# A fused decoder trunk on one core: the pooling chunk of the input projection moved among the attention tasks

## The chip, the cores and the metric

The kernel runs on one core of a Trainium2 chip. Its time is device microseconds (us) of that core for one launch, from host arrays to the finished output. Five engines work side by side, each through its own queue in program order: TensorE (PE, matrix products and transposes), VectorE (DVE), ScalarE (ACT), GpSimd (POOL) and SyncE (SP, which issues the transfers). They meet only at semaphores.

## What is computed

Two layers over a sequence of 512 with width 1024, all in float32. The part that matters here is one layer's mixer:

```python
proj = jnp.einsum('btd,dn->btn', x, w_in[l])
(qa, ka, va, u, qc, kcm, vcm, ksl, vsl, kwi, vwi, gc) = jnp.split(proj, offsets, axis=-1)
...
o_a = diff_attention(qa[:, :, 0], qa[:, :, 1], ka[:, :, 0], ka[:, :, 1], va, lam, lam_init, subln_g[l])
o_b = pool_mixer(u, w_pool[l], pool_scale[l])
qc = apply_rope(qc...); kcm = apply_rope(...); ksl = apply_rope(...); kwi = apply_rope(...)
o_c = nsa_attention(qc, kcm, _to_kv(vcm, B, T), ksl, _to_kv(vsl, B, T), kwi, _to_kv(vwi, B, T), gates, ...)
mix = jnp.einsum('btm,md->btd', jnp.concatenate([o_a, o_b, o_c], axis=-1), w_out[l])
x = layer_norm(ALPHA * x + mix, ln1_g[l], ln1_b[l])
```

Behind it stands a squared-ReLU MLP of width 4096 with its own layer norm. Mixer A is differential attention (queries `qa`, keys `ka`, values `va`), mixer B averages `u` over windows of 2 to 16 rows and multiplies by a small matrix, mixer C is attention with a compressed, a selected and a window branch.

## The kernel before

**Products.** Every large product is made of three TensorE products of high and low parts (lines 650 to 652, in the MLP's "up" also 646 to 648), so that float32 accuracy is kept. Weights come in units of 256 rows. SP loads a unit into a ring of four (`raw`), ScalarE writes its high part (`w_hi`, line 936), GpSimd the low part (`w_lo`, line 506), and TensorE gives the place free (`unit_used`) when it has used it. A chunk is four units, that is a block of columns against all 1024 rows, 96 matrix instructions for the four row tiles.

**Projection.** The input projection has seven chunks: the queries of A, the keys of A (384 columns each), the compressed keys and values of C (274 columns), the queries of C (384), the values of A (384), `u` (256), and a last chunk of 512 columns (the remaining keys and values of C and the gates). Six of them run back to back; the last one is cut in eight pieces of 12 instructions that stand between the first nine tasks of mixer A (`last_chunk`). ScalarE copies each chunk's banks out (`copy_in`, lines 973 and 980), VectorE turns the rotary embedding (`rotate`, lines 402 to 412): first queries and keys of A, then the compressed keys, then the queries of C.

**Early transposes.** `turn_early` (line 827) transposes eight 128-column pieces for later use, four of them halfway through the chunk of A's values, four halfway through the chunk of `u`. It waits for the rotations (`roped_a`, `roped_m`). ScalarE copies four of the results (line 988), VectorE four (line 1261). GpSimd then lays out rows for the compression (`rows_to_compress`, line 539).

**Tasks.** 36 tasks follow, 18 of A and 18 of C. For task t TensorE writes the scores of task t+2 (lines 691 to 705), turns the probabilities (`turn_p`, line 717) and multiplies with the values (lines 738, 753). VectorE takes the maximum (line 1271) and scales (lines 1301 to 1319), ScalarE does the exponentials (line 1060) and copies the turned probabilities (line 1069). A table `SIDE` says at which task which small step runs: compression, further transposes, the windows of mixer B (`box`), its small matrix (`pool`), the sums of squares, the compressed scores. ScalarE and VectorE empty these from PSUM at the next task, and every engine takes its queue strictly in order.

## Time and profile before

| | us |
|---|---|
| median of 3 runs | 1332.22 |
| lowest and highest | 1332.1, 1334.91 |
| the profiled execution | 1336.63 |
| its span, first to last instruction | 1334.8 |

All times below are read from the one profiled execution, from its span's start. The two layers do the same work; the second one's mixer comes about 660 us after the first one's, so that a place in the first layer stands for its twin.

### The profile page before, as it was taken

The numbers are of one execution on the slowest core, as the hardware profiler recorded it, in microseconds if no ns is written. First come the engines' busy times: TensorE is split into PE (matmuls) and PEld (weight loads), VectorE is DVE, ScalarE is ACT, GpSimd is POOL, SyncE is SP. The second block draws the span as 40 slices with busy tenths as digits, with TensorE's granted clock in tenths as the row PEclk, the third lists the DMA queues.
The fourth block names the chain that finished last, engine by engine and source line by source line (L and its number), as shares of the span: only waits on it lengthen the run. The fifth ranks groups of instructions, "written<-read, shape, count | busy, mean of one in ns | idle before, by whom it ended". The sixth has DMA issues, their size and how long they took to land.

```text
span 1334.8 us, 17810 instructions
## 1 busy us (share of the span) xinstructions
PE 1273.2 (95%) x7090; PEld 1048.9 (79%) x7090; DVE 741.3 (56%) x1115; ACT 482.3 (36%) x960; POOL 538.4 (40%) x300
## 2 busy tenths in 40 slices
PE   7999989998999999999989999899989999999996
PEld 7997755678888888888889967556888888888885
DVE  4485578448865072360486755884487632614516
ACT  5324567533322122221233345775323322212221
POOL 4464122043644444444354722210554444444444
PEclk9998999999999999999989999999999999999998
DMA  7432002031432323333134220010324323232311
GB/s 245 124 82 77 1 1 64 2 126 33 158 95 95 96 101 104 95 95 91 36 98 128 83 64 0 16 50 0 126 77 139 100 96 95 95 95 96 101 57 63
DMA packets 68833, 110.08 MB, mean 82 GB/s; under 512 B 15056, under 2 KB 27664, under 8 KB 68624
## 3 DMA queue, kind: packets, MB, share of 16 engines
q1 hardware_dynamic: 67600, 104.77, 25.4%
q10 hardware_dynamic: 1152, 4.19, 0.9%
q8 instruction: 56, 0.92, 0.3%
q14 instruction: 25, 0.20, 0.1%
HBM read 106.85 MB, written 2.10 MB: 82 GB/s over the span
## 4 chain that ended last, share of the span: by engine, by line
PE 89%; DVE 7%; ACT 2%; POOL 1%; DMA 0%; issue 0%; POOLq 0%; SPq 0%; DVEq 0%; ACTq 0%
PE ps L650 17%; PE ps L651 16%; PE ps L652 16%; PE ps L646 9%; PE ps L647 9%; PE ps L648 9%; PE ps L705 4%; PE ps L717 2%; PE ps L753 2%; DVE negmax L1271 1%; PE ps L605 1%; DVE probs L1319 1%; PE ps L738 1%; DVE xres L1180 1%; PE ps L779 1%; DVE probs_a L1319 1%
## 5 line engine op out<-in xcount | busy, mean ns | idle before, releaser
L506 POOL TENSOR_TENSOR w_lo<-raw,w_hi 128x1024 fp32r<-128x1024 f32 (+3 forms) x200 | 461.7, 2315 | 635.5 <-ACT w_hi L936 635.2
L936 ACT ACTIVATE w_hi<-raw 128x1024 fp32r<-128x1024 f32 (+3 forms) x200 | 198.3, 994 | 601.9 <-PE ps L652 363.2
L646 PE MATMUL ps<-xt_hi,w_lo 128*128 128x512 f32 (+1 forms) x576 | 212.1, 368 | 8.8 <-DVE xt_lo L1161 8.8
L648 PE MATMUL ps<-xt_lo,w_hi 128*128 128x512 f32 (+1 forms) x576 | 211.8, 368 | 0.0
L647 PE MATMUL ps<-xt_hi,w_hi 128*128 128x512 f32 (+1 forms) x576 | 211.7, 368 | 0.0
L650 PE MATMUL ps<-w_hi,xt_lo 128*128 128x384 f32 (+3 forms) x448 | 153.5, 343 | 7.8 <-DVE xt_lo L1161 4.4
L650 PE MATMUL ps<-w_hi,mt_lo 128*128 128x512 f32 x384 | 150.6, 392 | 3.8 <-DVE mt_lo L1324 3.0
L651 PE MATMUL ps<-w_hi,xt_hi 128*128 128x384 f32 (+3 forms) x448 | 150.2, 335 | 0.0
L652 PE MATMUL ps<-w_lo,xt_hi 128*128 128x384 f32 (+3 forms) x448 | 150.0, 335 | 0.0
L652 PE MATMUL ps<-w_lo,mt_hi 128*128 128x512 f32 x384 | 149.5, 389 | 0.0
L651 PE MATMUL ps<-w_hi,mt_hi 128*128 128x512 f32 x384 | 149.4, 389 | 0.0
L646 PEld LDWEIGHTS ps<-xt_hi,w_lo 128*128 128x128 f32 x576 | 109.7, 190 | 27.2 <-DVE xt_lo L1161 8.1
L648 PEld LDWEIGHTS ps<-xt_lo,w_hi 128*128 128x128 f32 x576 | 109.9, 191 | 17.3
L647 PEld LDWEIGHTS ps<-xt_hi,w_hi 128*128 128x128 f32 x576 | 109.7, 190 | 17.5
L1271 DVE TENSOR_REDUCE negmax<-ps 128x2 f32<-128x256 f32 (+2 forms) x96 | 76.8, 820 | 67.3 <-PE ps L705 67.1
L1378 DVE TENSOR_TENSOR xres<-xres,ps 128x512 f32<-128x512 f32 x48 | 32.9, 685 | 137.4 <-PE ps L652 136.6
L650 PEld LDWEIGHTS ps<-w_hi,xt_lo 128*128 128x128 f32 x448 | 86.2, 192 | 21.3 <-issue 11.0
L650 PE MATMUL ps<-w_hi,he_lo 128*128 128x512 f32 x256 | 99.6, 389 | 0.0
L651 PE MATMUL ps<-w_hi,he_hi 128*128 128x512 f32 x256 | 99.6, 389 | 0.0
L652 PE MATMUL ps<-w_lo,he_hi 128*128 128x512 f32 x256 | 99.6, 389 | 0.0
L1406 DVE TENSOR_TENSOR mt_lo<-tmp,mt_hi 128x512 fp32r<-128x512 f32 x32 | 71.3, 2229 | 47.9 <-ACT mt_hi L1136 47.9
L1414 DVE TENSOR_SCALAR tmp<-ps 128x512 f32<-128x512 f32 x64 | 44.1, 689 | 89.6 <-PE ps L648 88.5
(167 smaller groups left out, 1937.7 us busy)
## 6 DMA issues: line engine op xcount, KB each, us to landing
raw<-in_w_up SPq DMA_DIRECT2D x64, 512.0 KB, 3.7
raw<-in_w_down SPq DMA_DIRECT2D x64, 512.0 KB, 3.7
raw<-in_w_in SPq DMA_DIRECT2D x32, 384.0 KB, 3.3
raw<-in_w_in SPq DMA_DIRECT2D x8, 512.0 KB, 3.6
raw<-in_w_out SPq DMA_DIRECT2D x8, 512.0 KB, 3.3
raw<-in_w_out SPq DMA_DIRECT2D x12, 256.0 KB, 3.7
raw<-in_w_in SPq DMA_DIRECT2D x8, 274.0 KB, 2.9
xres<-in_x SPq DMA_DIRECT2D x4, 512.0 KB, 5.6
```

The source lines that it names most:

```text
L506: nc.gpsimd.tensor_tensor(unit_of(w_lo, u), unit_of(raw, u), unit_of(w_hi, u).bitcast(F32), ALU.subtract).then_inc(s_lo_ready, 1)
L646: mm(o, wl[:, c], a_hi[:, k, cols], start=first, stop=False)
L647: mm(o, wh[:, c], a_hi[:, k, cols], start=False, stop=False)
L648: return mm(o, wh[:, c], a_lo[:, k, cols], start=False, stop=end)
L650: mm(o, a_lo[:, k, c], wh, start=first, stop=False)
L651: mm(o, a_hi[:, k, c], wh, start=False, stop=False)
L652: return mm(o, a_hi[:, k, c], wl, start=False, stop=end)
L705: last = mm(o[:, at_:at_ + n], queries, keys, start=False, stop=True, skip_group_check=True)
L936: A(unit_of(w_hi, u), unit_of(raw, u), ACT.Copy).then_inc(s_hi_ready, 1)
L1271: last = V.tensor_reduce(negmax[:, t % 2, a, :], ps[:, b:b + 2, at_:at_ + n], AX.X, ALU.max, negate=True)
L1406: V.tensor_tensor(lo[:, f], tmp[:, f % 2], hi[:, f].bitcast(F32), ALU.subtract) \
L1414: link(V.tensor_scalar(tmp[:, f % 2], ps[:, bank + b, :], 0.0, None, ALU.max))
```

## The change

The chunk of `u` is no longer part of the run of chunks ahead of the tasks. The 512-column chunk (now `LATE`) comes as the sixth, cut into eight pieces, of which two now stand between the first two scores. The chunk of `u` (now `POOLED`) comes as the seventh, one row tile each at tasks 11, 13, 15 and 16. Since five chunks are left in the run, the early transposes move one chunk ahead. The steps of mixer B (`box`, `pool`) move from tasks 6 and 12 to tasks 18 to 22, one bank each. ScalarE empties `pool` and the sums of squares in VectorE's place, and takes the scale and the small constant into the logarithm. The compression runs as 32 products of 64x64 in place of 16 of 128x128.

```diff
-IN_COLS = ((0, 384), (384, 384), (O_KCM, 274), (O_QC, 384), (O_VA, 384), (O_U, 256), (O_KCM + 274, 512))
+IN_COLS = ((0, 384), (384, 384), (O_KCM, 274), (O_QC, 384), (O_VA, 384), (O_KCM + 274, 512), (O_U, 256))
-LAST = IN_CHUNKS - 1
+LATE, POOLED = IN_CHUNKS - 2, IN_CHUNKS - 1
+LATE_AT = {1: (1, 0), 2: (1, 1), 4: (2, 0), 5: (2, 1), 7: (3, 0), 8: (3, 1)}
+LATE_COPIED = {0: 0, 3: 1, 6: 2, 9: 3}
+POOLED_AT, POOLED_COPIED = {11: 0, 13: 1, 15: 2, 16: 3}, {12: 0, 14: 1, 16: 2, 17: 3}
...
+SIDE = {2: (("compress", 0, 5), ("turn", 7, 6)), 4: (("turn", 8, 5), ("turn", 9, 6)),
+        6: (("cmp_scores", 0, 5), ("cmp_scores", 1, 6)), 8: (("square_sums", 0, 5),), 12: (("turn", 11, 5), ("turn", 12, 6)),
+        14: (("cmp_turn", 0, 5), ("cmp_turn", 1, 6)), 16: (("square_sums", 1, 5),), 18: (("box", 0, LATE_BANK),),
+        19: (("box", 1, LATE_BANK),), 20: (("square_sums", 2, LATE_BANK),), 21: (("pool", 0, LATE_BANK),),
+        22: (("pool", 1, LATE_BANK),)}
...
# TensorE
-                    for j in range(16):
-                        last = mm(ps[:, bank, 0:P], cmp_wv[:, j].rearrange("p a e -> p (a e)"),
-                                  cmp_kw[:, j].rearrange("p a e -> p (a e)"), start=j == 0, stop=j == 15)
+                    for j in range(16):
+                        for kv in range(2):
+                            r = slice(64 * kv, 64 * kv + 64)
+                            last = mm(ps[r, bank, r], cmp_wv[:, j, kv, :], cmp_kw[:, j, kv, :], start=j == 0, stop=j == 15)
...
+            def pooled_tile(layer, b):
+                pe.wait_ge(s_in_copied, nth("in_copied", layer, TT * POOLED + b))
+                for k in range(KT):
...
+                    last = products(POOLED, k, b, LATE_BANK - b, xt_hi, xt_lo)
...
-                        gemm(layer, s, 4 * (k % 2), xt_hi, xt_lo, lambda kt: None, by_bank=k == LAST - 1,
-                             halfway=(lambda: turn_early(layer, k - 4)) if k >= 4 else None)
+                        gemm(layer, s, 4 * (k % 2), xt_hi, xt_lo, lambda kt: None, by_bank=k == LATE - 1,
+                             halfway=(lambda: turn_early(layer, k - 3)) if k >= 3 else None)
...
+                pe.wait_ge(s_in_copied, nth("in_copied", layer, TT * (LATE - 1) + 2))
                 scores(layer, 0)
+                late_piece(layer, 0, 0)
+                pe.wait_ge(s_in_copied, nth("in_copied", layer, TT * LATE))
                 scores(layer, 1)
+                late_piece(layer, 0, 1)
...
# ScalarE
-                    if 20 <= t < 24:
-                        split_to(layer, U_OUT + t - 19)
+                    if t in (20, 24, 28, 32):
+                        split_to(layer, U_OUT + t // 4 - 4)
...
+                    if t == 9:
+                        split_to(layer, U_OUT)
...
-                A(flat, flat, ACT.Ln).then_inc(s_chain_act, 1)
+                A(flat, flat, ACT.Ln, scale=1.0 / DV, bias=lams[:, 7:8]).then_inc(s_chain_act, 1)
...
# VectorE
+                copy_early(2)
+                copy_early(3)
                 dve.wait_ge(s_in_copied, nth("in_copied", layer, 4 * TT))
                 for tt in range(TT):
                     rotate(V.tensor_tensor, link, tt, ((T_QC, 6, 64, R_CCQ, R_SCQ),)).then_inc(s_roped_c, 1)
...
-                for n in (2, 3, 4, 6):
...
+                copy_early(4)
+                copy_early(6)
```

TensorE's queue at the first early transposes, in the first layer (before: rows 442 to 448 of the queue, in the chunk of A's values):

```order
L650 MATMUL ps<-w_hi,xt_lo 128x384
L651 MATMUL ps<-w_hi,xt_hi 128x384
L652 MATMUL ps<-w_lo,xt_hi 128x384
L827 MATMUL ps<-kc,proj_b 128x128 [waits in_copied,roped_m,roped_a]
L827 MATMUL ps<-kc,proj_b 128x128 x7
L827 MATMUL ps<-kc,proj_a 128x128 x8
L650 MATMUL ps<-w_hi,xt_lo 128x384 [waits hi_ready,lo_ready]
```

The same place after the change (rows 346 to 352, in the chunk of C's queries; the helper now has line 834):

```order
L658 MATMUL ps<-w_hi,xt_lo 128x384
L659 MATMUL ps<-w_hi,xt_hi 128x384
L660 MATMUL ps<-w_lo,xt_hi 128x384
L834 MATMUL ps<-kc,proj_b 128x128 [waits in_copied,roped_m,roped_a]
L834 MATMUL ps<-kc,proj_b 128x128 x7
L834 MATMUL ps<-kc,proj_a 128x128 x8
L658 MATMUL ps<-w_hi,xt_lo 128x384 [waits hi_ready,lo_ready]
```

The transposes and their wait for both rotations stand 96 matrix instructions, one chunk of 384 columns, earlier in the queue.

VectorE's queue from the last rotation of the compressed keys (`proj_b` 128x128) to the first score maximum, before:

```order
L412 TENSOR_TENSOR proj_b<-proj_b,tmp 128x384 [waits chain_dve]
L1261 COPY qa_64<-ps 128x512 [waits turned,roped_c]
L1261 COPY ka<-ps 128x512 [waits turned]
L1261 COPY qa_65<-ps 128x512 [waits turned]
L1261 COPY qa_66<-ps 128x512 [waits turned]
L1264 TENSOR_TENSOR lams<-lams 128x1 [waits lam_exp]
L1265 TENSOR_TENSOR lams<-lams,kc 128x1 [waits chain_dve]
L1271 TENSOR_REDUCE negmax<-ps 128x2 [waits scores,chain_dve]
```

And after, with the rotation of C's queries (`proj_b` 128x384, 16 rows) between the two pairs of copies:

```order
L419 TENSOR_TENSOR proj_b<-proj_b,tmp 128x128 [waits chain_dve]
L1295 COPY qa_65<-ps 128x512 [waits turned,roped_m]
L1295 COPY ka<-ps 128x512 [waits turned]
L409 TENSOR_TENSOR tmp<-proj_b,kc 128x6x32 [waits in_copied]
...
L419 TENSOR_TENSOR proj_b<-proj_b,tmp 128x384 [waits chain_dve]
L1295 COPY qa_66<-ps 128x512 [waits turned,roped_c]
L1295 COPY qa_67<-ps 128x512 [waits turned]
L1307 TENSOR_TENSOR lams<-lams 128x1 [waits lam_exp]
L1308 TENSOR_TENSOR lams<-lams,kc 128x1 [waits chain_dve]
```

Two copies now stand ahead of the rotation of C's queries, two behind it; the rotations of A's queries and keys and of the compressed keys keep their place.

ScalarE's queue at task 9 after the change, from the sums of squares to the exponentials of task 10 (`proj_k`, `proj_v`, `gates` are one row tile of the 512-column chunk, `w_hi` the four units of `u`):

```order
L1068 ACTIVATE rms<-ps 128x512 [waits side_ready]
L1007 ACTIVATE proj_k<-ps 128x110 [waits unit_used]
L1007 ACTIVATE proj_v<-ps 128x128
L1007 ACTIVATE proj_k<-ps 128x128
L1007 ACTIVATE proj_v<-ps 128x128
L1000 ACTIVATE gates<-ps 128x18
L963 ACTIVATE w_hi<-raw 128x2x256 [waits unit_used,raw0]
L963 ACTIVATE w_hi<-raw 128x2x256 [waits unit_used,raw1]
L963 ACTIVATE w_hi<-raw 128x2x256 [waits unit_used,raw2]
L963 ACTIVATE w_hi<-raw 128x2x256 [waits unit_used,raw3]
```

Before, no unit was split among the tasks of A; the sums of squares were VectorE's.

## Rows read from the trace of the kernel before

**Rows 1.** The page: engines' busy time, and the chain that ended last.

```profile
PE 1273.2 (95%) x7090; PEld 1048.9 (79%) x7090; DVE 741.3 (56%) x1115; ACT 482.3 (36%) x960; POOL 538.4 (40%) x300
...
PE 89%; DVE 7%; ACT 2%; POOL 1%; DMA 0%; issue 0%; POOLq 0%; SPq 0%; DVEq 0%; ACTq 0%
```

**Rows 2.** Windows: A's tasks in both layers, C's; PE first, PEclk after POOL.

```profile
110.30:197.20 86.90, 80.02 (x544) 55.66 (x542) 55.10 (x115) 46.84 (x156) 18.71 (x21) 0.94 0.07 19
197.20:254.40 57.20, 53.62 (x465) 32.73 (x465) 46.54 (x110) 45.16 (x116) 9.42 (x4) 1.00 0.13 38
770.60:855.90 85.30, 78.45 (x544) 54.84 (x542) 55.01 (x114) 46.79 (x156) 18.71 (x21) 0.96 0.07 20
```

**Rows 3.** TensorE's timeline, rows with idle time: start, us, engine, line, [idle <-releaser].

```profile
97.00 0.36 PE L650 MATMUL ps<-w_hi,xt_lo 128*128 128x256 f32 x1 [1.29 <-ACT proj_v L980]
...
114.52 0.34 PE L695 MATMUL ps<-mask,ident 128*128 128x128 bf16 x2 [1.77 <-ACT probs_a L1060]
...
189.44 1.32 PE L717 MATMUL ps<-kc,probs_a 128*128 128x128 f32 x6 [2.63 <-DVE probs_a L1317]
```

**Rows 4.** Windows: granted clock behind the wait of 1.77 us.

```profile
115.00:121.00 6.00, 6.00 (x15) 3.97 (x16) 4.07 (x11) 2.31 (x10) 0.65 (x1) 0.50 0.52 160
```

**Rows 5.** VectorE's timeline, rotations of the compressed keys, from its first row.

```profile
74.97 1.89 DVE L402 TENSOR_TENSOR tmp<-proj_b,kc 128x64 f32<-128x64 f32 x2
...
77.55 0.36 DVE L402 TENSOR_TENSOR tmp<-proj_b,kc 128x64 f32<-128x64 f32 x2
...
81.88 0.29 DVE L412 TENSOR_TENSOR proj_b<-proj_b,tmp 128x128 f32<-128x128 f32 x1
```

**Rows 6.** ScalarE's timeline: splits that mark used units, copies of C's queries.

```profile
69.06 0.85 ACT L936 ACTIVATE w_hi<-raw 128x768 fp32r<-128x768 f32 x1 [2.49 <-PE ps L652]
...
82.08 0.86 ACT L980 ACTIVATE proj_b<-ps 128x384 f32<-128x384 f32 x2
85.71 0.63 ACT L936 ACTIVATE w_hi<-raw 128x512 fp32r<-128x512 f32 x1 [2.77 <-PE ps L652]
```

**Rows 7.** GpSimd's timeline: a split beside the rotations, the next one.

```profile
69.99 1.87 POOL L506 TENSOR_TENSOR w_lo<-raw,w_hi 128x768 fp32r<-128x768 f32 x1 [2.11 <-ACT w_hi L936]
74.15 2.50 POOL L506 TENSOR_TENSOR w_lo<-raw,w_hi 128x768 fp32r<-128x768 f32 x1 [2.29 <-ACT w_hi L936]
```

**Rows 8.** TensorE's timeline: both early transposes, values of a task, the compression.

```profile
85.45 1.04 PE L827 MATMUL ps<-kc,proj_b 128*128 128x128 f32 x8
...
102.83 1.91 PE L827 MATMUL ps<-kc,proj_a 128*128 128x128 f32 x16
...
127.43 0.88 PE L738 MATMUL ps<-pt_a,proj_v 128*64 128x128 f32 x12
128.24 3.84 PE L779 MATMUL ps<-cmp_kw,cmp_wv 128*128 128x128 f32 x32
```

**Rows 9.** VectorE's timeline: a rotation of C's queries, and a copy behind it.

```profile
91.83 1.61 DVE L402 TENSOR_TENSOR tmp<-proj_b,kc 128x192 f32<-128x192 f32 x2
...
95.50 0.69 DVE L1261 COPY qa<-ps 128x512 f32<-128x512 f32 x1
```

**Rows 10.** ScalarE and TensorE: scores, exponentials, copies, transposes among tasks of A.

```profile
106.20 0.38 ACT L980 ACTIVATE proj_b<-ps 128x256 f32<-128x256 f32 x1 [0.83 <-PE ps L652]
...
132.55 1.13 PE L705 MATMUL ps<-ka,qa 32*128 32x512 f32 x4
133.48 0.68 ACT L1060 ACTIVATE probs_a<-ps,negmax 128x512 f32<-128x512 f32 x1
...
136.47 0.82 PE L717 MATMUL ps<-kc,probs_a 128*128 128x128 f32 x6
...
137.33 0.81 ACT L1069 ACTIVATE pt_a<-ps 128x768 f32<-128x768 f32 x1 [2.40 <-PE ps L717]
...
143.73 0.27 ACT L980 ACTIVATE proj_k<-ps 128x110 f32<-128x110 f32 x1
...
144.41 0.43 ACT L1060 ACTIVATE probs_a<-ps,negmax 128x128 f32<-128x128 f32 x1
```

More of the change, by code:

```diff
@@ L544, in _ @@
             for layer in range(DEPTH):
-                split(layer, 2 if layer else 0, U_LAST - 2)
+                split(layer, 2 if layer else 0, U_LATE - 2)
                 pool.wait_ge(s_const_in, 32)
@@ L570, in _ @@
                 rope_k(3)
+                split(layer, U_POOLED, U_OUT)
                 pool.wait_ge(s_cmp_factor, nth("cmp_factor", layer, 1))
@@ L828, in turn_early, with late_piece @@
                     last.then_inc(s_turned, 1)
-            def last_chunk(layer, t):
-                b = t // 3
-                if t % 3 == 0:
-                    pe.wait_ge(s_in_copied, nth("in_copied", layer, TT * LAST + b if b else TT * (LAST - 1) + 1))
-                for k in range(4 * (t % 3), 4 * (t % 3) + 4):
+            def late_piece(layer, b, half):
+                if b and not half:
+                    pe.wait_ge(s_in_copied, nth("in_copied", layer, TT * LATE + b))
+                for k in range(4 * half, 4 * half + 4):
                     if b == 0 and k % 2 == 0:
-                        pe.wait_ge(s_lo_ready, nth("lo_ready", layer, U_LAST + k // 2 + 1))
-                        pe.wait_ge(s_hi_ready, nth("hi_ready", layer, U_LAST + k // 2 + 1))
-                    last = products(LAST, k, b, LAST_BANK - b, xt_hi, xt_lo)
+                        pe.wait_ge(s_lo_ready, nth("lo_ready", layer, U_LATE + k // 2 + 1))
+                        pe.wait_ge(s_hi_ready, nth("hi_ready", layer, U_LATE + k // 2 + 1))
+                    last = products(LATE, k, b, LATE_BANK - b, xt_hi, xt_lo)
                     if b == 3 and k % 2:
@@ L842, in last_chunk @@
                     elif k == KT - 1:
-                        last.then_inc(s_last_done, 1)
+                        last.then_inc(s_late_done, 1)
+            def pooled_tile(layer, b):
+                pe.wait_ge(s_in_copied, nth("in_copied", layer, TT * POOLED + b))
+                for k in range(KT):
+                    if b == 0 and k % 2 == 0:
+                        pe.wait_ge(s_lo_ready, nth("lo_ready", layer, U_POOLED + k // 2 + 1))
+                        pe.wait_ge(s_hi_ready, nth("hi_ready", layer, U_POOLED + k // 2 + 1))
+                    last = products(POOLED, k, b, LATE_BANK - b, xt_hi, xt_lo)
+                    if b == 3 and k % 2:
+                        last.then_inc(s_unit_used, 1)
+                    elif k == KT - 1:
+                        last.then_inc(s_pooled_done, 1)
             pe.wait_ge(s_ident_in, 16)
@@ L849, in _ @@
                     turn_half(0, 0, 0)
-                for k, s in enumerate(range(LAST)):
+                for k, s in enumerate(range(LATE)):
                     if k >= 2:
@@ L887, in _ @@
                 for t in range(TASKS):
+                    if t == 16:
+                        pooled_tile(layer, POOLED_AT[t])
                     if t + 2 < TASKS:
                         scores(layer, t + 2)
-                    if t < 3 * TT and t % 3 < 2:
-                        last_chunk(layer, t)
+                    if t in LATE_AT:
+                        late_piece(layer, *LATE_AT[t])
+                    if t in POOLED_AT and t != 16:
+                        pooled_tile(layer, POOLED_AT[t])
                     if t == TASKS - 1:
@@ L994, in _ @@
                 act.wait_ge(s_const_in, 32)
-                for n in range(1, U_LAST - 1):
+                for n in range(1, U_LATE - 1):
                     if n == 4:
@@ L1039, in side_step @@
                         last = A(cmp_pt[0:64, 2 * c:2 * c + 2, 1, :], src[0:64, :, 1, :], ACT.Copy)
+                    elif kind == "square_sums":
+                        last = A(rms[:, c], b, ACT.Copy)
+                    elif kind == "pool":
+                        last = A(pooled[:, c], b, ACT.Identity, scale=psc[:, c:c + 1], bias=lams[:, 6:7])
                     elif kind == "box":
@@ L1220, in _ @@
             V.memset(lams[:, 6:7], 0.0)
+            V.memset(lams[:, 7:8], RMS_EPS)
             V.memset(kcmp[:], 0.0)
@@ L1276, in side @@
                     for n, (kind, c, bank) in enumerate(SIDE[t]):
-                        if kind in ("cmp_scores", "square_sums", "pool"):
+                        if kind == "cmp_scores":
                             dve.wait_ge(s_side_ready, nth("side_ready", layer, SIDE_FIRST[t] + n + 1))
```

131 lines of the change are left out of this document (64 added, 67 removed).

## The prediction

> **What bounds the kernel now.** I read the page first: TensorE is busy for 95% of the span and makes 89% of the chain that ended last [rows 1]. The reader is to see that no other engine is near it, so a change pays only where TensorE waits or runs slow. Then the windows of the stretch that is touched. The tasks of A take 86.9 us in the first layer with TensorE busy for 80.0, and 85.3 with 78.5 in the second; the tasks of C take 57.2 with 53.6 [rows 2]. So 6.9 us of waiting per layer stand in A and 3.6 in C. The granted clock there averages 0.94 and 0.96 [rows 2]: 0.06 x 86.9 = 5.2 us and 0.04 x 85.3 = 3.4 us of lost speed. A window shows where it goes: the clock stands at 0.50, the 1.2 GHz level, from 115 to 121 [rows 4], right behind a wait of 1.77 us for the exponentials of the first task [rows 3], 3.0 us lost; the other 2.2 us fit the other long wait, 2.63 us, where VectorE is late with task 15 [rows 3]. One wait stands ahead of the tasks, 1.29 us before the chunk of `u` [rows 3]. The row names ScalarE; by the wait's list and the time it is VectorE's second copy behind the rotation, which starts 0.6 us after the copy at 95.50 [rows 9]. All that the change can win, if it wins all of A and the wait ahead of it, is 6.9 + 5.2 + 1.3 = 13.4 us in the first layer and 6.9 + 3.4 + 1.3 = 11.6 in the second, 25.0 in all; C has 3.6 more per layer.
>
> **What moves at no price.** The chunk of `u` is 96 instructions; half of it runs from 97.00 to 102.83 [rows 3, 8], so it is 11.7 us of TensorE, taken from the projection and given to the tasks: nothing on a full TensorE except what it covers. The same holds for `box` and `pool`, which move to C. VectorE's five evacuations go to ScalarE, which is busy for 46.8 of 86.9 us in A and 45.2 of 57.2 in C [rows 2]; I cost them at nothing in C, where TensorE gets 4 us of new work to cover them, and take up to 2 us per layer either way for the range. The compression takes 3.8 us for 32 instructions, 0.12 each; with a 64-column operand the values' products take 0.81 to the next row for 12, 0.07 each [rows 8], and 64 of them are 4.3 us, while pairs that ran fully side by side at half the width would be 1.9. I take no change, and -1.9 to +0.5 per layer for the range. The scale in the logarithm, the later splits of the output weights and the transfers (whose order by unit stays) lie beside TensorE's work: nothing.
>
> **The cost: the early transposes come before their rotations are done.** They now stand halfway through the chunk of C's queries. The unit ahead of them was used at 69.06, where ScalarE's split starts, and the transposes start about 0.26 ahead of such a split (85.45 against 85.71), so TensorE arrives at 68.8 [rows 6, 8]. They wait for both rotations. VectorE, whose order up to there is the same, starts the compressed keys only at 74.97 and ends them at 82.17 [rows 5]. Before, that left 3.3 us of slack; now TensorE stands still. Its stop also stops GpSimd: the splits follow used units, the one at 69.99 ends at 71.9 and the one at 74.15 no longer comes [rows 7]. Beside it the first pair of multiplications took 1.89 us, without a split 0.36 [rows 5], so each row tile then takes the 1.05 us from 77.55 to 78.60 and the rotation ends at 74.97 + 4 x 1.05 = 79.2. TensorE waits from about 69.0 to 79.2: 10.2 us per layer, 13.2 if the slow pairs stay. Waits of 1.8 and 2.6 us cost 2.2 to 3.0 us by the clock in the first layer, (3.4 for both in the second) [rows 2 to 4]; this one should cost as much, part of it while TensorE stands anyway: 1.7 to 3.3 us, I take 2.
>
> The Trainium skill, "SBUF — State Buffer", "Who interferes with whom", says that VectorE with two inputs in SBUF and GpSimd reading SBUF shut each other out for whole instructions; 1.89 against 0.36 agrees, and by it the end is 79.2 and not 82.2. The skill's "TensorE: Matmul & The Clock Gate", "Part 4: PE-mode transpose", says that transposes do not count as busy for the clock. By that the 16 transposes behind the wait would not help it up, and the loss would be nearer 3.3 than 1.7; no row here separates transposes from products.
>
> **Behind it the second rotation is late too.** C's queries end 10 to 12 us later in the run and ScalarE's copies with them. Before, the transposes came 3 us after the copies ended at 82.9, and the rotation behind these copies took until 95.50 [rows 6, 9]. From 69.06 to 85.71 one chunk of 384 columns passes, 16.65 us [rows 6], and 16 transposes take 1.8 [rows 8]. Now the chunk ends at 79.2 + 1.8 + 8.3 + 2 = 91.3, the last copies as far behind it as before, 82.9 - (69.06 + 8.3) = 5.6, at 97. GpSimd then lays out its rows and splits up to about 106, so two row tiles take the contended 3.67 us (91.83 to 95.50 [rows 9]) and two perhaps 2.5 and 2 (an estimate: the rotation without a split beside it); VectorE ends at 109, and its two copies (0.7 each [rows 9]) at 110.5 to 111.2. The chunk of A's values ends at 91.3 + 16.6 + 1.8 = 109.7, and the first scores wait for the copies: 1.4 us. The two tiny steps of `lams` and the first maximum follow, covered by the first pieces of the 512-column chunk, which are 2.9 us each (133.6, where the scores at 132.55 end, to the transposes at 136.47 [rows 10]).
>
> **Among the tasks of A** ScalarE's order decides. At task 0 it now waits for the piece, copies a row tile (143.73 to 144.41, 0.7) and only then makes the exponentials of task 1, four of the kind at 144.41 (about 1.5), while TensorE has some 1.1 us of scores like those at 132.55: wait 1.3, and I take 1.4 with the latencies. At task 3 the transposes (136.47 to 137.13, 0.7) and scores (1.3) have no piece behind them, against the end of a copy, a row tile of 0.7 and exponentials of 2 x 0.67 [rows 10], 2.8 in all with their gaps: 0.8. At task 9 ScalarE empties the sums (0.5, like other 128x512 work of its own), copies a row tile (0.7), splits all four units of `u` (4 x 0.6, by the 128x512 split of 0.63 [rows 6]) and makes the exponentials of task 10 (1.35), 5.0 us against TensorE's 2.0: wait 3.0, and 0.5 behind it. At task 16 the tile of `u` waits for a copy of 0.81 and one of 0.38 [rows 10]: 1.3. At task 18 some 0.4. That is 7.4 us in the place of 6.9: the new products fill the old waits, and the rest opens others. The two long ones bring the clock down once or twice: 3 us.
>
> **The sum,** per layer: new 10.2 + 2 + 1.4 + 7.4 + 3 = 24.0, gone 13.4 and 11.6. So +10.6 and +12.4, in all +23.0 us. Against the profiled execution's 1336.6 that is 1359.6; its own time lies 4.4 above the median shown, so 1332.2 + 23.0 = 1355.2.
>
> **The rivals.**
> 1. Only the first stall counts (chance 0.22). For it: ScalarE has slack in A on average [rows 2], and if it is ahead at tasks 0 and 9 the waits halve to 3.7 with no further fall of the clock. Against it: the copies stand ahead of the exponentials in its queue. 10.2 + 2 + 1.4 + 3.7 = 17.3 per layer, against 25.0: +9.6, 1342.
> 2. ScalarE becomes the bound of the tasks (chance 0.13). For it: five evacuations more, and in C it is busy for 79% of the time already [rows 2]. Every step of C from 18 to 22 then adds some 0.6 us, the clock falls after each long wait (6 us in place of 3) and stays low for the longest time behind the stall (3.3 for 2): +7.3 per layer on the forecast, 1370.
> 3. Faster (chance 0.04): the pieces of products cover every wait. Its place is ScalarE's queue at tasks 0, 9 and 16: if the exponentials there are done when TensorE wants them, no wait of A is left and those of C go too. Then 10.2 + 2 + 1.4 = 13.6 per layer stand against 13.4 + 3.6 and 11.6 + 3.6: -5.0, 1327. It decides at new waits of 3.6 - 1.1 = 2.5 us per layer; above that the kernel is slower. Against it are the rows of each of these queues.
> 4. The stall does not come, since VectorE would be done by 69 (chance 0.03): it would need the rotations 10 us sooner, and nothing ahead of them moves. Then 1.4 + 7.4 + 3 = 11.8 against 12.5 on average, 1331: no change.
>
> The forecast has the remaining 0.58. Terms at their ends: the first stall 9.8 to 13.2 with a clock loss of 1.7 to 3.3, the second 0.5 to 3, A's waits 4 to 9 and clock 0 to 6. Not all fall to one side; the likeliest case alone spans 1346 to 1366. With rival 1 in it and most of rival 2 the range is 1339 to 1369. A difference of 0.2%, 2.7 us, is about what a measurement of this kernel can tell from none. Faster by more 0.04, within it 0.04, slower 0.92.
>
> **What would show it.** Right: an idle time of about 10 us on TensorE ahead of the first row of line 834 in both layers, released by VectorE's rotation of the compressed keys; half clock behind it; a wait of 1 to 3 us ahead of the first scores; waits on ScalarE's exponentials ahead of the scores of tasks 3, 6 and 12; no wait left at task 15 of A. The first pair of the compressed keys' rotation at 0.36 us. Wrong: no idle time at line 834, or an A stretch with under 3 us of waiting.

## The result, and the profile after

The changed kernel takes 1381.37 us (median of 4 runs, 1379.33 to 1383.92), the kernel before 1333.57 beside it (4 runs, 1332.10 to 1335.72). The two medians are 47.8 us apart. The ratio on record is 1.0338 with an interval of 1.0320 to 1.0355, which is 45 us, and the two profiled spans are 44.3 apart; the kernel before had medians from 1333.6 to 1337.5 in its sets of runs, so that differences of medians below are good to some 3 us. The forecast was 1355, slower by 23, with a range of 1339 to 1369. The direction and the first place are right, the size is half, and the time lies outside the range.

Three rows of the page, the span, the engines' busy time and the chain that ended last, against [rows 1]:

```profile
span 1379.1 us, 17939 instructions
...
PE 1284.4 (93%) x7154; PEld 1056.3 (77%) x7154; DVE 727.8 (53%) x1106; ACT 487.3 (35%) x970; POOL 539.4 (39%) x300
...
PE 85%; DVE 7%; ACT 3%; issue 2%; POOL 1%; DMA 1%; SPq 0%; POOLq 0%; ACTq 0%; DVEq 0%
```

The span grew by 44.3 us, TensorE's busy time by 11.2. It has 64 instructions more, and busy time also counts what runs at half clock. The other 33 us are standing, and "issue 2%", some 28 us, is new in the chain: time in which TensorE waited for something that the profile doesn't name.

TensorE's timeline, every row of the first layer's tasks and of what stands ahead of them that has 1 us or more of idle time in front, answering [rows 3]:

```profile
79.70 1.94 PE L834 MATMUL ps<-kc,proj_b 128*128 128x128 f32 x8 [10.21 <-issue]
...
115.77 0.38 PE L699 MATMUL ps<-mask,ident 128*128 128x256 bf16 x2 [4.51 <-issue]
...
128.12 0.28 PE L703 MATMUL ps<-mask,ident 128*128 128x128 bf16 x2 [1.57 <-ACT probs_a L1091]
...
144.89 0.39 PE L699 MATMUL ps<-mask,ident 128*128 128x256 bf16 x2 [1.09 <-ACT probs_a L1091]
...
176.25 0.39 PE L699 MATMUL ps<-mask,ident 128*128 128x256 bf16 x2 [2.86 <-ACT probs_a L1091]
...
203.71 0.39 PE L658 MATMUL ps<-w_hi,xt_lo 128*128 128x256 f32 x1 [1.17 <-ACT proj_u L1007]
...
240.02 1.54 PE L723 MATMUL ps<-kc,probs 128*128 128x128 f32 x6 [2.41 <-DVE probs L1355]
...
257.05 1.09 PE L723 MATMUL ps<-kc,probs 128*128 128x128 f32 x8 [1.67 <-DVE probs L1355]
```

Up to 203.71 these are the early transposes, the first scores and A's tasks; the two at line 723 are C's. The second layer has the same waits (10.20 ahead of 762.07, 4.50, 1.57, 1.09, 2.86, 1.18, 2.41, 1.68).

Windows over the stretches in which the granted clock is low in the first layer, answering [rows 4] (PE busy first, PEclk behind POOL):

```profile
72.00:86.00 14.00, 6.30 (x26) 6.33 (x27) 8.51 (x25) 1.29 (x3) 3.56 (x7) 0.51 0.12 37
115.80:120.30 4.50, 4.50 (x18) 3.06 (x19) 1.95 (x4) 1.72 (x8) 0.74 (x1) 0.62 0.34 90
130.00:134.00 4.00, 4.00 (x14) 3.07 (x13) 2.17 (x6) 0.00 (x0) 0.00 (x0) 0.57 0.00 0
177.00:185.00 8.00, 7.80 (x47) 5.95 (x44) 7.79 (x14) 3.69 (x13) 4.25 (x4) 0.57 0.86 237
239.00:247.00 8.00, 6.98 (x36) 4.61 (x38) 5.19 (x13) 3.78 (x11) 0.82 (x1) 0.57 0.24 66
```

Five falls to the 1.2 GHz level up to C's end, against two before, and each stands at one of the long waits above: 10.21, 4.51, 1.57, 2.86 and 2.41. At the first the clock is down from 72, while TensorE stands, and stays down until 86, over the transposes and the start of what follows.

VectorE's timeline at the two waits in front of the tasks, answering [rows 5, 9]:

```profile
75.45 0.36 DVE L409 TENSOR_TENSOR tmp<-proj_b,kc 128x64 f32<-128x64 f32 x2
...
79.31 0.29 DVE L419 TENSOR_TENSOR proj_b<-proj_b,tmp 128x128 f32<-128x128 f32 x1
...
98.97 1.18 DVE L409 TENSOR_TENSOR tmp<-proj_b,kc 128x192 f32<-128x192 f32 x2 [14.89 <-ACT proj_b L1007]
...
103.29 2.65 DVE L415 TENSOR_TENSOR proj_b<-proj_b,kc 128x384 f32<-128x384 f32 x1
105.97 2.63 DVE L419 TENSOR_TENSOR proj_b<-proj_b,tmp 128x384 f32<-128x384 f32 x1
...
111.16 0.56 DVE L415 TENSOR_TENSOR proj_b<-proj_b,kc 128x384 f32<-128x384 f32 x1
111.75 2.60 DVE L419 TENSOR_TENSOR proj_b<-proj_b,tmp 128x384 f32<-128x384 f32 x1
114.38 1.29 DVE L1295 COPY qa<-ps 128x512 f32<-128x512 f32 x2
```

The compressed keys are rotated from 75.45 to 79.60, and TensorE's transposes start at 79.70. C's queries are rotated from 98.97 to 114.35, the two copies end at 115.67, and the first scores start at 115.77. So both "issue" waits seem to have VectorE behind them, though the profile names nobody; the runs below test it. GpSimd's timeline beside it shows where the 2.6 us instructions come from:

```profile
103.01 5.18 POOL L513 TENSOR_TENSOR w_lo<-raw,w_hi 128x1024 fp32r<-128x1024 f32 x2
111.45 5.10 POOL L513 TENSOR_TENSOR w_lo<-raw,w_hi 128x1024 fp32r<-128x1024 f32 x2 [3.25 <-ACT w_hi L963]
```

The additions and multiplications that meet a split take 2.60 to 2.65 us, the same ones outside it 0.56 (109.31 and 111.16). The last one, at 111.75, meets the split at 111.45, which starts because the chunk of A's values has begun to free its units. The opening says that the engines meet only at semaphores. These rows show another meeting: VectorE's instruction itself gets longer beside GpSimd's.

**The accounting.** I add TensorE's idle times of 0.3 us or more, and for the clock what was lost in each microsecond: its busy time times one minus the granted clock. This is an estimate; over one pair of kernels below it comes out 2 us too high.

| us, first layer / second | before | after | change |
|---|---|---|---|
| waits ahead of the tasks | 1.3 / 1.3 | 14.7 / 14.7 | +13.4 / +13.4 |
| waits among A's tasks | 6.4 / 6.4 | 6.7 / 6.7 | +0.3 / +0.3 |
| waits among C's tasks | 3.9 / 3.9 | 5.8 / 5.8 | +1.9 / +1.9 |
| lost at half clock, up to C's end | 4.9 / 3.4 | 12.9 / 11.3 | +8.0 / +7.9 |
| the compression (3.84 before) | | 2.04 | -1.8 / -1.8 |
| sum | | | +21.8 / +21.7 |
| the same instruction, after less before | | | +22.9 / +21.7 |

The last line follows one instruction, the first of line 658 behind C (270.25 before, 293.12 after; 929.0 and 973.6 in the second layer, less what the first had given). The second layer's sum is complete. Of the 1.1 us that the first layer's lacks, 0.5 is older than the change's first wait: the chunk of C's queries starts at 60.97 for 60.45, since the first transfer came 0.5 us later in this execution and TensorE waited 0.99 for a split at 14.3. The other 0.6 is not traced. Over the whole program the clock's loss is 29.6 us against 14.1, and the idle time of 0.3 us or more behind 60 us is 71.8 against 40.6.

### The profile page after: what moved, and what is told of

The parts are those of the page before. It is cut to its first block, busy times and chain, and to the rows that moved or that the text cites. A ratio compares the mean times of both kernels' runs of the same rounds, so it can differ in the third digit from the quotient of the medians.

```text
span 1379.1 us, 17939 instructions
## 1 busy us (share of the span) xinstructions
PE 1284.4 (93%) x7154; PEld 1056.3 (77%) x7154; DVE 727.8 (53%) x1106; ACT 487.3 (35%) x970; POOL 539.4 (39%) x300
## 4 chain that ended last, share of the span: by engine, by line
PE 85%; DVE 7%; ACT 3%; issue 2%; POOL 1%; DMA 1%; SPq 0%; POOLq 0%; ACTq 0%; DVEq 0%
PE ps L658 16%; PE ps L659 15%; PE ps L660 15%; PE ps L654 8%; PE ps L655 8%; PE ps L656 8%; PE ps L713 4%; PE ps L723 3%; PE ps L759 2%; DVE tmp L409 1%; PE ps L744 1%; DVE proj_a L415 1%; PE ps L613 1%; DVE probs L1355 1%; PE ps L834 1%
## 5 line engine op out<-in xcount | busy, mean ns | idle before, releaser
L658 PE MATMUL ps<-w_hi,xt_lo 128*128 128x384 f32 (+3 forms) x448 | 156.6, 350 | 8.5 <-DVE xt_lo L1199 4.4
```

What stands on the lines that cost most here:

```text
L658: mm(o, a_lo[:, k, c], wh, start=first, stop=False)
```

## The experiments

Each ran beside the kernel before on the same chip, so its ratio is against that: medians of before were 1337.5 in the first four, 1337.0 with the parts put into before alone, 1336.4 in the rest. Theory 1 is the forecast's: VectorE is late at the early transposes, and the rest follows. What was open was how much each wait costs once its share of the clock is with it. The changed kernel itself was not run again beside them.

### Half of the rotation left out: what holds the first transposes

```
 for tt in range(TT):
-    rotate(... A's queries and keys ...).then_inc(s_roped_a, 1)
+    if tt < 2:
+        V.memset(tmp[:, 0, 0:1], 0.0).then_inc(s_roped_a, 1)
+    else:
+        rotate(... A's queries and keys ...).then_inc(s_roped_a, 1)
```

> The changed kernel with the rotation of A's queries and keys left out for two of the four row tiles (a tiny write stands in its place), so that VectorE is done about 11 us earlier. Theory 1, the transposes wait for VectorE's rotations: the 10.2 us wait of TensorE at line 834 goes in both layers, with the 2.85 us lost to half clock behind it, so 2 x 13 = 26 us less than the changed kernel, about 1355. Theory 2, the time comes back at the first scores, since VectorE's second rotation waits for ScalarE's copies: the wait of 4.5 us there grows and only some 10 to 15 us are won, about 1369.

Measured: 1369.83 us (1364.82 to 1376.98), ratio 1.0243 (1.0202 to 1.0285). The four runs lie 12 us apart, and the profiled one is the fastest. Its span is 16.1 us shorter than the changed kernel's. The wait fell to 4.44, not to nothing. VectorE's timeline:

```profile
64.44 0.96 DVE L419 TENSOR_TENSOR proj_a<-proj_a,tmp 128x768 f32<-128x768 f32 x1
66.83 1.22 DVE L409 TENSOR_TENSOR tmp<-proj_b,kc 128x64 f32<-128x64 f32 x2 [1.43 <-ACT proj_k L1007]
...
70.18 1.91 DVE L415 TENSOR_TENSOR proj_b<-proj_b,kc 128x128 f32<-128x128 f32 x1
...
73.17 0.29 DVE L419 TENSOR_TENSOR proj_b<-proj_b,tmp 128x128 f32<-128x128 f32 x1
```

VectorE is through with A's rotation 10 us sooner (65.40 against 75.42) and then waits itself for the last copy of the compressed keys by ScalarE. Their rotation takes 6.6 us, with two instructions lengthened beside a split, and ends at 73.46; TensorE goes on at 73.56. So the early transposes have two conditions in a row, and with half the work VectorE still holds them for 4.4 us. That points to their place in the program, and not to one slow rotation. The next wait stayed as it was: 4.49 ahead of the first scores, as in the full kernel. So the median lies near theory 2's number, but not for theory 2's reason.

### The wait filled with products: what the clock behind it costs

```
+if n == 0:
+    pe.wait_ge(s_in_copied, nth("in_copied", layer, 3 * TT))
+    for _ in range(42):
+        mm(ps[:, 0, :], xt_hi[:, 0, 0:P], xt_hi[:, 0, :], start=True, stop=True)
 pe.wait_ge(s_roped_a, nth("roped_a", layer, TT))
```

> The changed kernel with 42 products of 512 columns (0.227 us each, 9.5 us, into a bank that the transposes overwrite) ahead of the wait for VectorE's rotations at line 834; they fill the 10.2 us wait of TensorE and add nothing to the result. Theory 1, the half clock behind a wait comes from TensorE having stood still: the clock stays at full speed through the wait, the transposes start at the same time as before (79.7 us), and the 2.9 us lost behind it in each layer come back: 3 to 6 us in all, about 1377. Theory 2, the clock there falls for another reason: it stays at 0.50 and the time is 1381 or more.

Measured: 1379.25 us (1374.86 to 1380.36), ratio 1.0314 (1.0294 to 1.0335), about 2 us less than the changed kernel, and the two intervals overlap. TensorE's timeline:

```profile
69.10 9.72 PE L829 MATMUL ps<-xt_hi 128*128 128x512 f32 x42
79.58 1.06 PE L837 MATMUL ps<-kc,proj_b 128*128 128x128 f32 x8 [0.75 <-DVE proj_b L419]
80.47 1.04 PE L837 MATMUL ps<-kc,proj_a 128*128 128x128 f32 x8
```

Now the last wait, 0.75, is named: VectorE's addition at line 419, the compressed keys' rotation. The granted clock from 69 to 83 is 1.00, and eight transposes take 1.06 us where they took 1.94. Theory 1's cause holds, and so does the price on the spot: 3.0 us less lost in the first layer. But the whole span is only 0.5 us shorter (1378.6). The clock's loss over both layers is 28.7 against 29.6 in the changed kernel, though the 4.5 behind the two filled waits are gone, since other falls are longer this time: behind the 1.56 in the second layer the clock now falls from 806 to 814, 3.4 lost, where the changed kernel had no fall. A fall avoided at one wait is not simply subtracted; whether the falls that follow depend on it, or vary from one execution to the next, this run doesn't tell.

### Copies of the first scores ahead of the last two rotations

```
     for tt in range(TT):
         rotate(... C's queries, row tile tt ...)
         dve.wait_ge(s_roped_c, nth("roped_c", layer, tt + 1))
-    copy_early(4)
-    copy_early(6)
+        if tt == 1:
+            copy_early(4)
+            copy_early(6)
```

> The changed kernel with VectorE's two copies for the first scores ahead of the last two row tiles of the rotation of C's queries, not behind them. Theory 1, the 4.5 us wait ahead of the first scores is these copies' place in VectorE's queue: it goes, with the 1.7 us of half clock behind it, 12 us less in all, about 1369. Theory 2, the maximum of the first task then comes late (VectorE still rotates until about 115) and the wait moves to the scores of tasks 2 and 3: under 4 us less, about 1378.

Measured: 1369.37 us (1368.91 to 1372.25), ratio 1.0241 (1.0225 to 1.0256). The wait of 4.5 is gone from TensorE's timeline (no idle time over 0.3 between 80.1 and 120.8), and in place of the 1.57 stand 1.66 and 1.20 at the scores of tasks 2 and 3. VectorE's timeline shows why those came:

```profile
108.46 1.29 DVE L1295 COPY qa<-ps 128x512 f32<-128x512 f32 x2
...
111.50 4.88 DVE L409 TENSOR_TENSOR tmp<-proj_b,kc 128x192 f32<-128x192 f32 x2
...
117.99 1.95 DVE L1315 TENSOR_REDUCE negmax<-ps 128x2 f32<-128x256 f32 x4
```

The copies are done at 109.7, before TensorE wants them, but the rotation that is left runs into the same split (4.88 for a pair), and now the maxima of the first tasks stand behind it. Waits of 6.1 us per layer became 2.9; with 3.3 us less lost by the clock over both layers that is 9.7, and the span is 8.7 shorter. So the second wait was a term of its own, worth 9 to 13 us by span, median and ratio, and came from VectorE's order against GpSimd's splits.

### The early transposes back at the end of the projection

```
-TURN_EARLY = ((Q_KCM, 0), (Q_VCM, 1), (0, 2), (3, 3)), ((1, 4), (4, 5), (2, 6), (5, 7))
+TURN_EARLY = ((Q_KCM, 4), (Q_VCM, 5), (0, 6), (3, 7)), ((1, 4), (4, 5), (2, 6), (5, 7))
...
-halfway=(lambda: turn_early(layer, k - 3)) if k >= 3 else None)
+halfway=(lambda: turn_early(layer, 0)) if k == LATE - 1 else None,
+midway=(lambda: turn_early(layer, 1)) if k == LATE - 1 else None)
```

Both groups now stand in the chunk of A's values: the first halfway, the second behind its second bank. The copies behind them and GpSimd's rows move with them. VectorE's four copies also move in between its rotations, as in the run before this one, `kvcm` gets another place in memory, and ScalarE's wait for the rows of the compression comes one task later. So this run takes both waits away together and does not tell them apart.

> The changed kernel with both groups of early transposes in the chunk of A's values (halfway, and behind its second row tile), where the first group stood in the kernel before; GpSimd lays out the rows of the values first, splits the 512-column chunk and lays out those of the keys, and VectorE copies between its rotations. Theory 1, the two waits at the transposes and at the first scores (10.2 and 4.5 us per layer) are the change's only large price: both go with the half clock behind them (4.6 us), nothing takes their place, 2 x 19 us less, about 1343. Theory 2, GpSimd's split of the 512-column chunk or VectorE's rotation becomes the wait instead: 5 to 8 us of it come back per layer, about 1355.

Measured: 1346.30 us (1344.65 to 1347.91), ratio 1.0074 (1.0059 to 1.0089). Windows of TensorE's stretch that held both waits, and TensorE's rows behind it:

```profile
60.00:108.00 48.00, 46.56 (x277) 43.05 (x275) 44.80 (x63) 17.03 (x41) 30.37 (x23) 1.00 0.30 87
```

```profile
105.58 0.50 PE L658 MATMUL ps<-w_hi,xt_lo 128*128 128x512 f32 x1 [0.66 <-POOL w_lo L513]
108.41 0.28 PE L705 MATMUL ps<-mask,ident 128*128 128x128 bf16 x2 [1.19 <-ACT probs_a L1090]
110.74 0.40 PE L705 MATMUL ps<-mask,ident 128*128 128x128 bf16 x2 [1.20 <-ACT probs_a L1090]
```

In the stretch TensorE is busy for 46.6 of 48 us at the 2.4 GHz level. Per layer 16.3 us of waits (10.2, 4.5 and 1.57) became 3.05, which is 26.5 for both; the clock's loss fell from 29.6 to 19.5, 10.1 more. Together 36.6, against a span shorter by 34.6: TensorE's busy time fell by only 8.1, so the estimate of the clock's part is 2 us too high. The move with all that goes with it is worth 35 us, by the medians and by the ratios. It is not an exact return: before, the second group stood in the chunk of `u`, which now comes among the tasks.

### Two edits on the splits

```
-if t == 9:
-    split_to(layer, U_OUT)
+if t in (8, 9, 10):
+    split_to(layer, U_POOLED + {8: 2, 9: 3, 10: 4}[t])
```

> The changed kernel with ScalarE's splits of the four units of u at tasks 8 (two), 9 and 10 in place of all four at task 9. Theory 1, ScalarE's queue at task 9 makes TensorE wait 2.86 us for the exponentials of task 10, and the clock falls behind it (3.4 us lost in the first layer, more in the second): the wait shrinks to about 1.1 us and the clock stays up, 4 to 6 us less per layer, about 1371. Theory 2, the clock falls there for the sum of short waits before it, not for this one: 1.7 us per layer, about 1378.

Measured: 1379.82 us (1377.80 to 1383.65), ratio 1.0320 (1.0300 to 1.0341), within the changed kernel's own scatter. ScalarE's timeline in the changed kernel shows the queue that the forecast had worked out, 171.46 to 176.19:

```profile
171.46 0.60 ACT L1068 ACTIVATE rms<-ps 128x512 f32<-128x512 f32 x1 [4.08 <-PE ps L797]
...
172.63 2.23 ACT L963 ACTIVATE w_hi<-raw 128x512 fp32r<-128x512 f32 x4
174.71 0.72 ACT L1091 ACTIVATE probs_a<-ps,negmax 128x512 f32<-128x512 f32 x1
```

With the four splits over three tasks the wait of 2.86 became 1.30 and 0.98 (1.30 alone in the second layer), but the clock fell there all the same (176 to 184 and 855 to 866). The wait was ScalarE's, as forecast; shortening it to 1.3 did not save the clock.

```
-if t in (20, 24, 28, 32):
-    split_to(layer, U_OUT + t // 4 - 4)
+if 20 <= t < 24:
+    split_to(layer, U_OUT + t - 19)
```

> The changed kernel with the splits of the output weights back at tasks 20 to 23, in place of 20, 24, 28 and 32. In the changed kernel GpSimd's low part for task 24's unit meets VectorE's scaling of the probabilities (3.10 us for the group in place of 1.01) and TensorE waits 2.41 us, with half clock behind it for 6.5 us. Theory 1, it is that collision's place in the task (a task of two short tiles, whose scaling is four instructions) that makes the long wait: with the old places the waits in C are those of the kernel before (3.3 us and no fall of the clock), 1 to 5 us less per layer, about 1375. Theory 2, each split costs its collision wherever it stands: no change, 1381.

Measured: 1374.92 us (1373.60 to 1376.97), ratio 1.0279 (1.0264 to 1.0294). This takes up C's wait of 2.41. In the changed kernel GpSimd's split for the output weights lies at 237.45, and VectorE's timeline beside it reads:

```profile
236.87 3.10 DVE L1355 TENSOR_SCALAR probs<-probs,facs 128x128 f32<-128x128 f32 x4
...
241.76 1.01 DVE L1355 TENSOR_SCALAR probs<-probs,facs 128x128 f32<-128x128 f32 x4
...
253.96 2.11 DVE L1348 TENSOR_TENSOR facs<-recs,gates 128x2 f32<-128x2 f32 x1
```

The four scalings of a task take 3.10 us beside a split and 1.01 without, and at 253.71 the next split holds even a product of 2 columns for 2.11. With the splits moved to tasks 20 to 23 the waits of 0.33, 2.41, 1.67 and 0.91 became 0.32, 0.62, 0.49, 0.42 and 0.90, and windows show C's stretch at full clock:

```profile
228.00:243.00 15.00, 13.64 (x120) 8.83 (x120) 14.32 (x30) 13.76 (x34) 4.88 (x2) 1.00 0.35 106
```

It is worth about 6 us of median, 4 of span. No fall of the clock is left in C in either layer, but others came or grew (one behind a wait of 1.08 at 143.6, a longer one behind 2.85), and the loss over the whole program is 30.9 against 29.6. So the gain in this execution is the waits', 5.1 us in both layers. The two edits and the transposes' move together:

> As a_turns_late, with the units of u split at tasks 8 to 10 and the output weights at tasks 20 to 23. If the waits add up as the single runs say (6 us for the output weights, 2 for the units of u), 6 to 10 us under a_turns_late, about 1334, no better than the kernel before with the compression in halves (1330.6). If the pieces of u in A's tasks are worth what they cover, it comes under 1328.

Measured: 1337.46 us (10 runs, 1335.41 to 1338.90), ratio 1.0004 (0.9994 to 1.0014): the time before. Waits sum to 39.0 against 40.6 before, the clock's loss to 18.0 against 14.1. So the three places make up the whole difference. What is left of the change holds the faster compression, which alone made the kernel before faster (1330.62, next section); the rest of it costs about as much as that wins, some 7 us by the two ratios.

### Parts of the change put into the kernel before

```
 for j in range(16):
-    last = mm(ps[:, bank, 0:P], cmp_wv[:, j]..., cmp_kw[:, j]..., start=j == 0, stop=j == 15)
+    for kv in range(2):
+        r = slice(64 * kv, 64 * kv + 64)
+        last = mm(ps[r, bank, r], cmp_wv[:, j, kv, :], cmp_kw[:, j, kv, :], start=j == 0, stop=j == 15)
```

> The kernel before with the compression alone as 32 products of 64x64. In the changed kernel these 64 instructions took about 2.4 us, where 32 of 128x128 took 3.8. Theory 1, they run side by side in pairs and the time is TensorE's: 1.4 us less per layer, 2.8 in all, about 1330.5. Theory 2, ScalarE behind it sets the pace there: under 1 us in all.

Measured: 1330.62 us (1328.71 to 1333.36), ratio 0.9953 (0.9940 to 0.9965): faster by 6.4. TensorE's timeline:

```profile
126.59 2.03 PE L781 MATMUL ps<-cmp_kw,cmp_wv 128*64 128x64 f32 x64
```

It took 3.84 [rows 8], so 1.8 per layer, near the low end that I had kept for the range. (The changed kernel's rows have 2.04 and 2.03, not the 2.4 of the expectation.) The span is 5.8 shorter: 3.6 by this, and 2.2 less lost by the clock (11.9 against 14.1). Next, the evacuations by ScalarE (the first condition is in its code, the second in VectorE's), alone and with the compression:

```
-if kind in ("turn", "box", "compress", "cmp_turn"):
+if kind != "cmp_scores":
...
-if kind in ("cmp_scores", "square_sums", "pool"):
+if kind == "cmp_scores":
```

The copies themselves move with the conditions, and ScalarE's logarithm takes the scale and the small constant, as in the changed kernel.

> The kernel before with ScalarE emptying pool and the sums of squares in VectorE's place, nothing else. Theory 1, VectorE was what TensorE waited for at tasks 13 and 15 (1.02 and 2.63 us, with 1.7 us of half clock behind): 1.3 us less work of VectorE there takes 2 to 4 us per layer away, about 1327. Theory 2, ScalarE's queue is as tight and the wait only changes its name: within 1 us of the kernel before.

> The kernel before with both: the compression in halves and ScalarE's evacuations. If the two are independent, the sum of both gains, about 1324; if one wait takes the place of the other, no better than the better one.

Measured: 1336.56 us (11 runs, 1335.84 to 1338.33), ratio 1.0000 (0.9992 to 1.0009), and with the compression 1332.22 (1331.46 to 1335.49), 0.9968 (0.9956 to 0.9980). TensorE's timeline with the evacuations on ScalarE:

```profile
176.64 0.28 PE L695 MATMUL ps<-mask,ident 128*128 128x128 bf16 x2 [0.92 <-ACT probs_a L1064]
178.28 1.27 PE L738 MATMUL ps<-pt_a,proj_v 128*64 128x128 f32 x16 [0.51 <-ACT pt_a L1073]
185.90 0.28 PE L695 MATMUL ps<-mask,ident 128*128 128x128 bf16 x2 [1.16 <-ACT probs_a L1064]
```

Before, this stretch had 1.02 and 2.63, both VectorE's. Now it has 0.92, 0.51 and 1.16 by ScalarE, 1.1 us less in the first layer, and C's waits are longer (0.73, 1.55 and 0.96 for 0.34, 1.25 and 0.75). The second layer has a wait of 1.00 for VectorE besides. Most of the waits changed their owner; the time did not move. With the compression the kernel is no better than with the compression alone (1332.22 and 1330.62), so the evacuations bring nothing there either.

### The faster compression, and the two long waits of A filled

```
+def busy(n):
+    for _ in range(n):
+        mm(ps[:, LAST_BANK, 0:256], ident, kc[:, K_FIRST:K_FIRST + 256], start=True, stop=True)
...
 scores(layer, 1)
+pe.wait_ge(s_in_copied, nth("in_copied", layer, TT * (LAST - 1) + 1))
+busy(4)
...
+if t == 15:
+    busy(5)
 turn_p(layer, t)
```

These products (two instructions each in the profile) go into a bank that is free there, and nobody reads them.

> The kernel before with the compression in halves, and idle products of TensorE in two of its waits per layer: 4 of 256 columns (0.45 us each) behind the second scores, 5 ahead of the turned probabilities of task 15; they write a free bank and add nothing to the result. Theory 1, the clock fell for these waits of 1.77 and 2.63 us: it stays up, 1.7 to 3.3 us less at each, about 6 us in all against 1330.6. Theory 2, they only delay what follows, or the clock falls for the sum of small waits: no gain.

Measured: 1326.87 us (1326.56 to 1328.36), ratio 0.9931 (0.9916 to 0.9945). It is the fastest kernel here, 9.5 us below the kernel before, and 3.7 below the one with the compression alone. The intervals of these two ratios overlap slightly, and no run of this one is as slow as the fastest of the other (1328.71). TensorE's timeline, and windows that take up [rows 4]:

```profile
113.01 1.99 PE L683 MATMUL ps<-kc 128*128 128x256 f32 x8
...
182.16 2.43 PE L683 MATMUL ps<-kc 128*128 128x256 f32 x10
184.88 0.88 PE L722 MATMUL ps<-kc,probs_a 128*128 128x128 f32 x6 [0.29 <-DVE probs_a L1327]
```

```profile
113.00:119.00 6.00, 6.00 (x32) 4.16 (x30) 5.13 (x15) 4.57 (x20) 3.00 (x2) 1.00 0.57 182
184.00:192.00 8.00, 7.45 (x63) 4.96 (x61) 7.49 (x19) 6.75 (x23) 0.00 (x0) 1.00 0.01 2
```

The waits have the length they had (1.77 and 2.63, now 1.99 of products, and 2.43 with 0.29 of waiting), but the clock stays at 1.00 behind both, where it had stood at 0.50 from 115 to 121 and, with the faster compression alone, at 0.67 from 188 to 192. The loss went from 11.9 to 7.1 us, and the span fell by 4.1. In the second layer the clock had fallen behind the first of the two waits only, not behind the second (2.64), so three falls went and not four. What is left lies at waits of 3.8 and 3.1 us outside the tasks.

## Why the prediction was half right

**What bounds the kernel**: right. TensorE stood 33 us longer and lost 15.5 more by its clock (the estimate of the accounting), less 3.6 for the compression: 45, against spans 44.3 apart.

**The first stall**: right in place, cause and size, 10.21 and 10.20 us against 10.2 (TensorE came at 69.5 for 69.0 and VectorE ended at 79.6 for 79.2, both with the start of the program, which was 0.5 later). The rotation of the compressed keys starts with the pair at 0.36, since GpSimd's next split no longer came [rows 7], and takes 4.2 us as forecast. What I had not seen is the second condition. ScalarE's last copy lets the compressed keys' rotation start at 66.83 at the earliest, and it took 6.6 us from there, so that the transposes were 4.4 us late even with half of A's rotation left out. The Trainium skill, "SBUF — State Buffer", "Who interferes with whom", has the rule that decided between 79.2 and 82.2, and both the pair's 0.36 us without a split and the 2.60 to 2.65 at 103 to 114 agree with it.

**The wait ahead of the first scores**: mechanism right, size wrong, 4.5 for 1.4. The step that failed is the length of the row tiles, "two row tiles take the contended 3.67 us" and the others "perhaps 2.5 and 2", on the view that GpSimd splits up to about 106. The pair of splits that starts at 103.01 ends at 108.2. But the chunk of A's values frees its units from 110 on, and each freed unit brings a split. The last addition of the rotation met it, 2.60 for 0.56. The second tile, 102.21 to 108.60, took 6.4 us where I had 3.67, and the last 3.9 for 2; the first and the third were 1.1 quicker together. That VectorE started 2 us later than I had it is nearly balanced by the chunk of A's values, which ended 1.6 later. I had used the rule on GpSimd for the first stall, and not followed the ring of units to the second.

**Among A's tasks**: right in the sum, 6.7 us of waits above 0.3 against 7.4, and at the named places: ahead of the scores of task 3, 1.57 (1.4 forecast), of task 6, 1.09 (0.8), of task 12, 2.86 (3.0), and at the tile of `u`, 1.17 (1.3). The wait at task 18 came too, 0.48 (0.4), and the table counts it with C. The 0.5 behind task 9 did not come.

**The clock**: the term that was mis-sized, and the largest part of the error. I took 2 us behind the first stall and 3 for A, 5 per layer. The trace has 12.9 and 11.3. In the first layer they are 3.0 behind the stall, 1.7 behind the second wait (I took none), 1.7 and 3.4 in A, and 3.1 in C (none). I had read the price of a fall about rightly from [rows 2 to 4], 1.7 to 3.3 us, and then let it apply to "once or twice". (The 2.2 us that I gave the second fall before were 1.7 in its own windows.) Every wait of 1.57 us or more up to the end of C in the first layer, except for the 1.67 at 257, came with a fall; in the second layer the waits of 1.57 and 1.68 had none. The run with filled waits shows that the fall hangs on TensorE's standing, and not on the work behind it: the same waits, kept busy, had a clock of 1.00.

**C**: forecast unchanged, and it is 1.9 us of waits and 3.1 of clock worse in the first layer. I costed the later splits of the output weights at nothing because they "lie beside TensorE's work". They do, but VectorE's scalings take 3.10 us beside them for 1.01, and VectorE's scaling is what C's transposes wait for. Moving the splits took 2.6 us of waits per layer and C's falls of the clock away, though falls elsewhere took the latter's place in that run.

**The compression**: taken at nothing, -1.8 per layer in fact, near the end of its range. It took the error down a little.

**The transposes and the clock.** The forecast left open whether the transposes behind a wait bring the clock back later, as one may read the Trainium skill, "TensorE: Matmul & The Clock Gate", "Part 4: PE-mode transpose", which says that they do not count as busy for the clock in the same way. The loss was 3.0 in the first layer and 1.5 in the second with the same 16 transposes there, and the changed kernel's second layer decides it. TensorE's timeline and windows behind its wait of 10.20 us:

```profile
763.80 1.65 PE L834 MATMUL ps<-kc,proj_a 128*128 128x128 f32 x8
765.21 0.42 PE L658 MATMUL ps<-w_hi,xt_lo 128*128 128x384 f32 x1
```

```profile
762.00:765.00 3.00, 2.93 (x14) 2.96 (x15) 0.03 (x1) 1.29 (x3) 0.17 (x2) 0.50 0.02 5
765.00:765.20 0.20, 0.20 (x4) 0.20 (x3) 0.20 (x1) 0.00 (x0) 0.20 (x1) 0.89 0.00 0
```

The clock is back, 0.89 on average from 765.00 to 765.20, before the first product starts at 765.21: since the wait TensorE had run nothing but transposes. The runs with the splits of `u` and of the output weights moved show the same in their second layers (clock up ahead of 763.31 and 762.72, transposes alone from 760.05 and 759.42). So here the transposes did bring the clock back, and the measurement goes against what the Trainium skill says there. In the run with the wait filled, 16 transposes on a clock at 1.00 (1.06 and 1.04 us) did not bring it down.

In numbers, the first layer: 10.6 forecast, 22.9 measured. The 12.3 between are 7.9 of clock after the change and 0.3 that the kernel before had less to give back, 3.1 ahead of the first scores, 1.9 in C and 1.1 outside these terms (0.5 of it from the program's start), less 0.2 in A and 1.8 for the compression. Rival 2 named more falls of the clock, but by another cause, ScalarE as the bound of C, and that did not happen.

## What to carry to other kernels

A stretch of work that was moved ahead of a producer brought three prices here and not one: the wait, the clock behind it, and the next hand-over that the delayed engine is late for. Six waits of 1.57 to 10.21 us in one layer brought five falls of the clock, each 1.7 to 3.4 us of speed: price a wait with its fall. Filling such waits with products that nobody needs paid some 4 us in one kernel and 0.5 (span) to 2 (median) in the changed one, where other falls grew. And where a split on GpSimd starts by itself when a unit is freed, look for what VectorE does at that moment: an instruction of 0.56 us took 2.60.

## What the runs showed of the hardware that I had not expected

- The fall of the clock did not shrink with the wait: 2.86 us and 1.30 with 0.98 us behind it both had a fall of 3.0 to 3.4 us lost in the first layer. And the same wait does not always bring a fall. In one execution of the changed kernel the wait of 1.57 had one in the first layer (1.7 lost) and none in the second; with the first wait filled, the second layer's had one too (3.4 lost) behind the same instructions.
- Transposes alone brought the clock back from the 1.2 GHz to the 2.4 GHz level, in the second layer of three kernels.
- Products of 64 columns for two halves of the array, issued in turn, ran in 2.03 us for 64 instructions, 0.032 each, against 3.84 for 32 whole ones, 0.120 each.
- GpSimd's split held back a VectorE instruction with two columns for 2.11 us (0.16 otherwise), and four scalings by a factor per row for 3.10 (1.01 otherwise).
